# A two-layer decoder trunk on one core: rows of their own for the decay factors, a tile by tile norm behind the second output projection, and ten identity products at the front

## The reference

```python
y = rmsnorm(h, g)                      # rsqrt(mean(h*h)) per token, times the gain
# mLSTM, one head: scores of q and k, weighted by a decay, then times v
qk = silu(causal_depthwise_conv(y @ w_qk, conv_w))
s = (q_t @ k_s) * exp(b_t - b_s + i_s - m_t)   for s <= t
h = h + mixer(y)                       # ends in  mixed @ w_out
h = h + (silu(y2 @ w_gate) * (y2 @ w_up)) @ w_down      # y2 = rmsnorm(h, g2)
```

## Time and profile before

| | |
|---|---|
| median of three runs | 1417.23 us (1416.01 to 1417.27) |
| profiled execution, its own time | 1413.36 us |
| its span, first to last instruction | 1411.6 us |
| mean granted TensorE clock | 0.983 of full speed |
| matmuls in flight | 96% of the span |
| DVE, ACT, POOL busy | 50%, 39%, 20% |
| DMA | 114.11 MB, mean 81 GB/s |

### The profile page before, as it was taken

One profiled execution on the slowest core, in us unless ns is written; L12 is line 12 of the kernel. 1 busy time (PEld: TensorE's weight loads), 2 busy tenths in 40 slices (PEclk: granted clock), 3 DMA queues, 4 the chain that ended last, 5 costly groups with the idle time before them and its releaser, 6 DMA issues.

```text
span 1411.6 us, 18054 instructions
## 1 busy us (share of the span) xinstructions
PE 1352.6 (96%) x6431; PEld 1060.6 (75%) x6431; DVE 708.7 (50%) x1258; ACT 550.5 (39%) x998; POOL 277.9 (20%) x268
## 2 busy tenths in 40 slices
PE   7999989999999999999999989997989999999998
PEld 6767677888888888888777854444878888888887
DVE  4459875644343433233889578766244434343222
ACT  4336654433333333232453346665243333332222
POOL 2046453121111111001265101112111111111010
PEclk9999999999999999999999999999999999999999
DMA  7322221223333333322333210000223333333321
GB/s 221 90 60 61 60 60 46 84 81 104 104 90 104 89 113 110 102 81 80 82 118 111 74 31 1 1 1 1 75 75 105 89 104 89 104 106 105 99 61 60
DMA packets 203944, 114.11 MB, mean 81 GB/s; under 512 B 5712, under 2 KB 200528, under 8 KB 203760
## 3 DMA queue, kind: packets, MB, share of 16 engines
q1 hardware_dynamic: 203264, 112.97, 27.3%
q0 software_dynamic: 416, 0.35, 0.3%
q10 hardware_dynamic: 208, 0.06, 0.0%
HBM read 111.27 MB, written 2.10 MB: 80 GB/s over the span
## 4 chain that ended last, share of the span: by engine, by line
PE 83%; DVE 8%; ACT 4%; issue 3%; POOL 2%; DMA 0%; DVEq 0%; POOLq 0%; SPq 0%; ACTq 0%
PE acc L574 23%; PE acc L575 23%; PE acc L576 23%; PE acc L1049 3%; PE aux L1036 2%; DVE w_low L481 1%; PE acc L1026 1%; PE aux L1026 1%; ACT w_high L462 1%; DVE cmp_in_low L1709 1%; ACT score L1448 1%; PE aux L961 1%; PE acc L1059 1%; PE acc L983 0%; PE acc L659 0%
## 5 line engine op out<-in xcount | busy, mean ns | idle before, releaser
L481 DVE TENSOR_TENSOR w_low<-raw,w_high 128x1024 fp32r<-128x1024 f32 (+1 forms) x187 | 250.6, 1340 | 533.0 <-ACT w_high L462 532.7
L574 PE MATMUL acc<-y_high,w_high 128*128 128x512 f32 x1056 | 421.1, 399 | 12.1 <-DVE w_low L473 6.4
L576 PE MATMUL acc<-y_high,w_low 128*128 128x512 f32 x1056 | 414.2, 392 | 0.0
L575 PE MATMUL acc<-y_low,w_high 128*128 128x512 f32 x1056 | 414.0, 392 | 0.0
L462 ACT ACTIVATE w_high<-raw 128x1024 fp32r<-128x1024 f32 (+1 forms) x187 | 206.9, 1107 | 346.0 <-PE acc L576 337.0
L574 PEld LDWEIGHTS acc<-y_high,w_high 128*128 128x128 f32 x1056 | 200.0, 189 | 57.3 <-DVE w_low L473 7.9
L576 PEld LDWEIGHTS acc<-y_high,w_low 128*128 128x128 f32 x1056 | 199.4, 189 | 43.0
L575 PEld LDWEIGHTS acc<-y_low,w_high 128*128 128x128 f32 x1056 | 200.1, 189 | 41.6 <-issue 0.7
L574 PE MATMUL acc<-ffn_high,w_high 128*128 128x512 f32 (+1 forms) x374 | 141.0, 377 | 0.0
L575 PE MATMUL acc<-ffn_low,w_high 128*128 128x512 f32 (+1 forms) x374 | 140.9, 377 | 0.0
L576 PE MATMUL acc<-ffn_high,w_low 128*128 128x512 f32 (+1 forms) x374 | 140.9, 377 | 0.0
(11 more groups left out here) (288 smaller groups left out, 1621.7 us busy)
## 6 DMA issues: line engine op xcount, KB each, us to landing
raw<-in_l_w_in_dram SPq DMA_DIRECT2D x44, 512.0 KB, 3.7
raw<-in_l_w_gate_dram SPq DMA_DIRECT2D x44, 512.0 KB, 3.7
raw<-in_l_w_up_dram SPq DMA_DIRECT2D x44, 512.0 KB, 3.7
raw<-in_l_w_down_dram SPq DMA_DIRECT2D x32, 704.0 KB, 4.5
raw<-in_l_w_out_dram SPq DMA_DIRECT2D x16, 512.0 KB, 3.5
x_rows<-in_x_dram SPq DMA_DIRECT2D x4, 512.0 KB, 5.6
raw<-in_l_cmp_w_k_dram SPq DMA_DIRECT2D x4, 512.0 KB, 3.8
raw<-in_l_cmp_w_v_dram SPq DMA_DIRECT2D x4, 512.0 KB, 3.7
```

The costliest lines, as they stand in the source:

```text
L481: dve.tensor_tensor(dst, src, high.bitcast(F32), ALU.subtract).then_inc(S("split_low"), 1)
L574: pe.matmul(o, ah, bh, start=first, stop=False)
L575: pe.matmul(o, ah, bl, start=False, stop=False)
L576: return pe.matmul(o, al, bh, start=False, stop=last)
```

## The change

Four edits.

1. Decay: a third buffer, `decay[2]`, four arena rows from 25 (those of `v_d`), for head 2 and, behind its 1280 columns, for rows of tiles 0 to 2 of head 3; the last row of head 3 goes into `step3`. Head h < 3 has `decay[h]`. `DECAY_AT` becomes (9, 15, 19, 23). Heads 2 and 3 wait on POOL for `o_sum` of 16, that is for the last values of the attention heads, in place of the `weigh` of the head two before. The exponential of head 3 becomes two instructions.
2. WO1: the turned head sums go to `oh` and `ol` (arena rows 8 to 15 and 16 to 23, until then `q_rot` and the doubled keys), the units read them there, and `y` is made tile by tile behind each unit, as behind WO0. What ACT and DVE do in WO0 stays as it was.
3. Front: ten products of the identity with 256 columns of constants, into a bank that nothing reads, behind the turn of `param_rows` and ahead of the first unit.
4. `feature_unit` takes the source of its right hand side as an argument.

```diff
-DECAY_AT = (9, 17, 21, 25)
+DECAY_AT = (9, 15, 19, 23)
...
-        decay = [row("decay0", 13, 3), row("decay1", 29, 3)]
+        decay = [row("decay0", 13, 3), row("decay1", 29, 3), row("decay2", 25, 4)]
...
+        oh, ol = row("o_high", 8, 8, F32R), row("o_low", 16, 8, F32R)
...
+        def decay_of(h, i):
+
+            if h == 3:
+                return sn[3] if i == 3 else decay[2][:, block_at(4) + block_at(i):block_at(4) + block_at(i + 1)]
+            return decay[h][:, block_at(i):block_at(i + 1)]
...
@@ block.tensor: front
+            for w in range(10):
+                pe.matmul(aux[:, 0, 0:256], ident, kc[:, 0:256], start=True, stop=True)
             for j in range(4):
                 token_unit(AT["VD", j], [("VD", i) for i in range(4)], j, True)
...
             for m in range(8):
-                feature_unit(FIRST["WO1"] + m, ("WO1", m))
+                feature_unit(FIRST["WO1"] + m, ("WO1", m), source=(oh, ol))
...
@@ block.scalar: post, WO0 and WO1
-                    if j == 7:
-
-                        wait_unit(act, u)
-                        for m in range(3):
-                            norm_y(n, m)
+                    wait_taken(act, (name, j))
+                    norm_y(n, j)
+                    if j == 7:
                         split_high(act, u + SPL)
-                    wait_taken(act, (name, j))
                     square(n, j)
-                    if j == 7:
-                        for m in range(3, KT):
-                            norm_y(n, m)
...
             def decay_exp(h):
                 act.wait_ge(S("m_log"), h + 1)
-                d = decay[h % 2][:, 0:block_at(4)]
+                if h < 3:
+                    d = decay[h][:, 0:block_at(4)]
+                else:
+                    d = decay[2][:, block_at(4):block_at(4) + block_at(3)]
+                    act.activation(sn[3], sn[3], ACT.Exp).then_inc(S("m_exp_last"), 1)
                 act.activation(d, d, ACT.Exp).then_inc(S("m_exp"), 1)
...
-                act.activation(yh.rearrange("p (m t) -> p m t", t=T)[:, 4 * half:4 * half + 4, col(i)],
+                act.activation(oh.rearrange("p (m t) -> p m t", t=T)[:, 4 * half:4 * half + 4, col(i)],
...
@@ block.vector: post, WO0 and WO1
-                    if (name, j) == ("WO0", 7):
-                        norm_low(1, 7)
+                    norm_low(1 + 2 * int(name[2]), j)
+                    if j == 7:
                         split_low(dve, u + SPL)
-                    elif j == 7:
-                        n = 1 + 2 * int(name[2])
-                        for m in range(3):
-                            norm_low(n, m)
-                        split_low(dve, u + SPL)
-                        for m in range(3, KT):
-                            norm_low(n, m)
-                    elif name == "WO0":
-                        norm_low(1, j)
...
@@ block.gpsimd
-                    pool.wait_ge(S("m_weight"), 4 * h - 4)
+                    pool.wait_ge(S("o_sum"), 16)
...
                 pool.wait_ge(S("m_exp"), h + 1)
+                if h == 3:
+                    pool.wait_ge(S("m_exp_last"), 1)
```

More of the change, by code:

```diff
@@ L579, in unit_split, with feature_unit @@
                 pe.wait_ge(S("split_low"), u + 1 + it * per)
-            def feature_unit(u, tile, y_ready=None, it=0, per=0, uses=0, mid=None):
+            def feature_unit(u, tile, y_ready=None, it=0, per=0, uses=0, mid=None, source=None):
                 s = u % SPL
+                high, low = source or (yh, yl)
                 unit_split(u, it, per)
@@ L588, in feature_unit @@
                         pe.wait_ge(S(y_ready[0]), y_ready[1] + k)
-                    mm = mm3(ps(tile)[:, :], wh[s][:, col(k)], wl[s][:, col(k)], yh[:, tcol(k)], yl[:, tcol(k)],
+                    mm = mm3(ps(tile)[:, :], wh[s][:, col(k)], wl[s][:, col(k)], high[:, tcol(k)], low[:, tcol(k)],
                              k == 0, k == KT - 1)
@@ L1188, in post @@
                     n = 1 + 2 * int(name[2])
-                    if name == "WO0":
-                        wait_taken(act, (name, j))
-                        norm_y(n, j)
-                        if j == 7:
-                            split_high(act, u + SPL)
-                        square(n, j)
-                        return
+                    wait_taken(act, (name, j))
+                    norm_y(n, j)
                     if j == 7:
-                        wait_unit(act, u)
-                        for m in range(3):
-                            norm_y(n, m)
                         split_high(act, u + SPL)
-                    wait_taken(act, (name, j))
                     square(n, j)
-                    if j == 7:
-                        for m in range(3, KT):
-                            norm_y(n, m)
                 elif name == "KC" and j == 0:
@@ L1848, in weigh @@
                 dve.scalar_tensor_tensor(out=sn[4 + n % 4][:, 0:w], in0=aux[:, n % 2, 0:w],
-                                         scalar=float(P) ** -0.5, in1=decay[h % 2][:, block_at(i):block_at(i) + w],
+                                         scalar=float(P) ** -0.5, in1=decay_of(h, i),
                                          op0=ALU.mult, op1=ALU.mult).then_inc(S("m_weight"), 1)
@@ L2084, in _ @@
                 dve.wait_ge(S("mix_high"), MIXED + q + 1)
-                dve.tensor_tensor(yl.rearrange("p (m t) -> p m t", t=T)[:, 4 * half:4 * half + 4, col(i)],
+                dve.tensor_tensor(ol.rearrange("p (m t) -> p m t", t=T)[:, 4 * half:4 * half + 4, col(i)],
                                   aux[:, 2 + q % 2, :].rearrange("p (m t) -> p m t", t=P),
-                                  yh.bitcast(F32).rearrange("p (m t) -> p m t", t=T)[:, 4 * half:4 * half + 4, col(i)],
+                                  oh.bitcast(F32).rearrange("p (m t) -> p m t", t=T)[:, 4 * half:4 * half + 4, col(i)],
                                   ALU.subtract).then_inc(S("mix_low"), 1)
@@ L2182, in decay_log @@
             def decay_log(h, i):
-                d = decay[h % 2]
+                d = decay_of(h, i)
                 if h == 0:
@@ L2189, in decay_log @@
                 else:
-                    pool.wait_ge(S("m_weight"), 4 * h - 4)
+                    pool.wait_ge(S("o_sum"), 16)
                 for s in range(i + 1):
-                    o = pool.tensor_scalar(d[:, block_at(i) + s * P:block_at(i) + (s + 1) * P],
+                    o = pool.tensor_scalar(d[:, col(s)],
                                            nmb[:, h * T + i * P:h * T + (i + 1) * P],
@@ L2200, in decay_cut @@
                 pool.wait_ge(S("m_exp"), h + 1)
+                if h == 3:
+                    pool.wait_ge(S("m_exp_last"), 1)
                 for i in range(TT):
-                    d = decay[h % 2][:, block_at(i) + i * P:block_at(i + 1)]
+                    d = decay_of(h, i)[:, col(i)]
                     o = pool.tensor_tensor(d, d, kc[:, K_TRI:K_TRI + P], ALU.mult)
```

## The result

The changed kernel takes 1391.01 us, the median of four runs (1389.45 to 1392.78); the kernel before 1416.62 us beside it (1412.57 to 1417.27, four runs). The ratio is 0.9837, 95% interval 0.9815 to 0.9859: 1.6% faster. The forecast was 1396.9 us and a gain of 20.3. The gain is 25.6 us between the medians, and 21.5 us between the two profiled executions (1413.36 and 1391.86 us, spans 1411.6 and 1389.7).

What follows compares the result with a forecast made beforehand. TensorE, with matmuls in flight for 96% of the span, was taken as the bound, time being won only at its idle or low-clock places; 2.3 + 13.8 + 4.2 = 20.3 us took 1417.23 to 1396.9 us, range 1391.5 to 1404.

Steps and rivals of the forecast that it cites:

- Front: Idle stretch before the first weights: ten products keep the clock high, making twelve slow matmuls fast; 2.3 us gained.
- The level was high at 11.7: Step at the front: TensorE's clock already rose during the transposes of x, which the products need for their gain.
- Rival (b): At the front: the clock is low at 11.7 or falls despite the products, no gain; 1399.2 us, chance 0.10.
- Decay rows: Three attention slots: the exponential moves out of the way of the key's silu, ending waits on qk_m; 13.8 us gained.
- the silu of the key comes in the next slot with nothing ahead of it: at 186.6: Step in ACT's slots: the silu starts at 186.6 to 187.3 against TensorE's need at 188.5, 1.2 us to spare.
- Rival (a): In the three slots: the decay stall only moves, 2 us a slot stay; 1402.9 us, chance 0.14.
- WO1: From WO1's last unit to the norm's rows: 15.87 us becomes WO0's 11.64, without waits for y_low; 4.2 us gained.
- Rival (d): Behind the second output projection: only the idle time is gained, 3.6 us; 1397.5 us, chance 0.02.
- (c): At m_log: POOL's additions for heads 1 to 3 come so late that ACT holds TensorE; slower, 1420 us, chance 0.02.

Runs made afterwards that it cites:

- x9: The changed kernel run again with nothing changed; its runs go from 1388.51 to 1393.44 us.
- x1: The changed kernel without the ten identity products at the front; median 1393.17 us.
- x2: The changed kernel with the decay rows, their times and their waits of the kernel before; 1407.86 us.
- x10: The changed kernel with the decay rows of its own but the old times (17, 21, 25); 1408.32 us.
- x4: The changed kernel with the two old decay buffers and the waits on m_weight, but the new times (15, 19, 23); 1402.39 us.
- x7: The changed kernel with the silu of a key put ahead of the head work in ACT's slots 10, 12, 14 and 16; 1387.39 us.
- x3: The changed kernel with layer 1's second norm again made behind the last unit of WO1; median 1394.53 us.
- x5: The changed kernel with thirty transposes of 128 columns at the front in place of the ten products; median 1390.58 us.
- x11: The changed kernel with five products at the front in place of ten; stretch 0 to 2 is 9.80 us, 1.61 more.
- x8: x7 with four identity products in each of two waits for w_low in layer 1's projection; 1386.98 us.

## Why the prediction was right, and where its sizes were off

**The total.** Faster, as forecast with 0.96. The median of 1391.01 us lies half a microsecond under the range, 1391.5 to 1404 (its lower end, by the terms that I gave for it, 1396.7 - 5.6, should have been 1391.1); the ratio on the median that I started from, 0.9837 x 1417.23, is 1394.2, inside it. The sum of the three terms was 20.3 us and the traces show 2.35 + 12.97 + 4.25 = 19.6. What the medians have on top of it is not in any term: 2.0 us of low clock in places that change from trace to trace (x9), 0.25 us by which x came in earlier, and the profiled executions, that of the kernel before 3.3 us faster than its median and that of the changed kernel 0.9 us slower. That the medians come out 5 us better than the forecast is luck, not a term. I took the sum off the median as it was, and did not ask how far the runs of such a kernel spread. Its clock falls in six places between 700 and 990 us, and its runs on record go from 1408.6 to 1418.0 us.

**Front.** Right step by step: 4.3 to 4.55 us of products (4.49), end at 16.0 to 16.3 (15.94, with x in 0.25 us earlier), 2.3 us gained (2.35; x1: 2.42). The level was high at 11.7, as the short loads of the last transposes said. The ten products show it too: twenty instructions in 4.49 us, 0.22 each, with nothing but transposes ahead of them. Rival (b) falls.

**Decay rows.** The mechanism was right: the exponential and its two tables left the way of the key's silu, and with the wait went the low clock behind it (x2, x10). The term was 0.8 us too large. The step that failed is "the silu of the key comes in the next slot with nothing ahead of it: at 186.6": there is `head_rows` ahead of it, and I took `head_rms` at its usual 0.55 us, ready in time. I had moved POOL's additions and not asked what `head_rms` then falls beside. It fell beside DVE's split, took 1.62 us, and my 1.2 us to spare became 0.2 us of waiting, in two of three slots. Rival (a) came true at an eighth of its price, 0.8 of 6 us; x4 shows it in full. x7 shows that the order on ACT was the remaining cause: with the silu ahead of `head_rows` both slots take 7.99 us, though `head_rms` is as slow as before. That this rival stayed small is in part luck: its 1.4 us of waiting met 1.2 us to spare.

**WO1.** 4.2 forecast, 4.25 measured, 4.21 in x3; taking the same stretch behind WO0 as the price of the new form was exact. Rival (d), a gain of the idle time alone, falls; so does (c).

## What to carry to other kernels

Price a wait of TensorE by the whole stretch that holds it against one like it without it: here 8.3 us of waits cost 13.9 us by the rows of before, and 13.0 to 15.1 in the comparisons. Where another place of the same kernel already has the new form, its row is the best estimate there is. And an instruction moved on a helper engine is to be laid beside what the other engines do at its new time, not only beside its own queue.

## What the runs showed of the hardware that was not expected

- A one-column instruction of POOL, `head_rms`, takes 0.56 us alone and 1.61 to 1.65 us when it begins together with DVE's split, which has two SBUF inputs and takes 1.22 us. In all traces together there are twenty such slow ones, begun between 0.01 us ahead of the split and 0.03 us behind it; one begun nearly 0.03 us ahead, in the kernel before, took 0.56 (shown under x2). But the addition of 1.80 us in x4 had begun 0.08 us ahead, so no distance in time can be read from these traces as a safe one. No run moved one of the two instructions alone. The Trainium skill names the contention: by "GPSIMD Engine Reference", section "1. Specifications", DVE instructions with two SBUF inputs are among those that contend with POOL. The traces agree.
- Transposes kept TensorE's clock up here as products did (x5: 1.00, stretch 0 to 2 of 8.21 us against 8.19), and the level rose while TensorE did nothing but the transposes of x (loads of 226 ns, then 141).
- In x11 the low level followed an idle gap of 2.2 us, but behind the restart: full clock in the gap and for the first four matmuls, low from 17.2 us. The granted clock of the gap itself does not show what it costs. Not every such gap is followed by it: of the waits of 2.3 and 2.1 us in layer 1's projection one was in the first trace of the changed kernel, the other in x9, and both in x7.
- One short place of low clock through which TensorE works cost 1.6 us (x11; stretch 10 to 12 in x9). Whether it comes at a given place differs between executions of one code, so a gain by filling a gap is read from its own stretch (front, x8), and a gain of the whole only from many runs.
